# Moving a layer's modulation products from TensorE to VectorE, into three feed-forward stages

## What is computed

```
mod_lat = silu(c) @ w_mod + b_mod          # c: (1, 1024), w_mod: (1024, 6144)
mod_ctx = silu(c_ctx) @ w_mod + b_mod
sh1, sc1, g1, sh2, sc2, g2 = split(mod_lat, 6)
csh1, csc1, cg1, csh2, csc2, cg2 = split(mod_ctx, 6)
hx = modulate(rms_norm(x), sh1, sc1)
hc = modulate(rms_norm(ctx), csh1, csc1)   # with one layer nothing else of mod_ctx is used
```

## Time and profile before

| what | value |
|---|---|
| time, median of 3 runs | 2467.96 us (2465.76 to 2468.3) |
| span of the profiled execution, first to last instruction | 2465.7 us |
| mean granted clock of TensorE | 0.959 |
| PE busy | 2246.6 us, 91% |
| PEld busy | 2014.1 us, 82% |
| DVE busy | 979.8 us, 40% |
| ACT busy | 1157.1 us, 47% |
| POOL busy | 1191.6 us, 48% |

### The profile page before, as it was taken

One profiled execution on the slowest core, in us unless ns is written; L12 is line 12 of the kernel. 1 busy time (PEld: TensorE's weight loads), 2 busy tenths in 40 slices (PEclk: granted clock), 3 DMA queues, 4 the chain that ended last, 5 costly groups with the idle time before them and its releaser, 6 DMA issues. The chain is left out here.

```text
span 2465.7 us, 41821 instructions
## 1 busy us (share of the span) xinstructions
PE 2246.6 (91%) x17916; PEld 2014.1 (82%) x17916; DVE 979.8 (40%) x1980; ACT 1157.1 (47%) x1651; POOL 1191.6 (48%) x304
## 2 busy tenths in 40 slices
PE   8998989899998999888989999897987777998998
PEld 7998865488998999785568999775866777998997
DVE  2321644324211220356242321256665777333540
ACT  5433632465433442543255543455883555553342
POOL 6774610074875877440053887332310000675784
PEclk9999999899999999999989999898998888999999
DMA  7554522253654555432333554331204111653552
GB/s 251 171 175 130 155 83 86 69 173 101 201 170 143 189 183 162 139 111 86 120 103 103 171 188 154 118 104 52 69 21 135 35 36 24 209 165 126 180 180 95
DMA packets 303958, 318.49 MB, mean 129 GB/s; under 512 B 7881, under 2 KB 295101, under 8 KB 303261
## 3 DMA queue, kind: packets, MB, share of 16 engines
q1 hardware_dynamic: 303773, 315.81, 39.8%
HBM read 312.58 MB, written 3.21 MB: 128 GB/s over the span
## 5 line engine op out<-in xcount | busy, mean ns | idle before, releaser
L370 POOL TENSOR_TENSOR slab_lo<-ring,slab_hi 128x2048 fp32r<-128x2048 f32 (+1 forms) x238 | 1073.5, 4527 | 762.7 <-ACT slab_hi L359 727.0
L359 ACT CAST slab_hi<-ring 128x2048 fp32r<-128x2048 f32 (+1 forms) x238 | 443.8, 1869 | 550.8 <-PE bank L440 278.8
L435 PE MATMUL bank<-ffn_h_hi,slab_hi 128*128 128x256 f32 x1344 | 331.2, 284 | 0.0
L436 PE MATMUL bank<-ffn_h_lo,slab_hi 128*128 128x256 f32 x1344 | 329.7, 283 | 0.0
L435 PEld LDWEIGHTS bank<-ffn_h_hi,slab_hi 128*128 128x128 f32 x1344 | 257.9, 192 | 0.5 <-issue 0.3
L436 PEld LDWEIGHTS bank<-ffn_h_lo,slab_hi 128*128 128x128 f32 x1344 | 258.0, 192 | 0.1
L402 PE MATMUL bank<-ffn_hidden_hi,slab_hi 128*128 128x256 f32 x704 | 199.3, 283 | 0.0
L403 PE MATMUL bank<-ffn_hidden_lo,slab_hi 128*128 128x256 f32 x704 | 199.2, 283 | 0.0
L404 PE MATMUL bank<-ffn_hidden_hi,slab_lo 128*128 128x256 f32 x704 | 199.2, 283 | 0.0
L440 PE MATMUL bank<-ffn_h_hi,slab_lo 128*128 128x256 f32 x1344 | 189.1, 283 | 4.4 <-POOL slab_lo L370 4.4
L440 PEld LDWEIGHTS bank<-ffn_h_hi,slab_lo 128*128 128x128 f32 x1344 | 173.3, 192 | 5.2 <-POOL slab_lo L370 5.2
(11 more groups left out here) (655 smaller groups left out, 5369.0 us busy)
## 6 DMA issues: line engine op xcount, KB each, us to landing
ring<-in_ffn_w_in SPq DMA_DIRECT2D x88, 1024.0 KB, 5.1
ring<-in_ffn_w_out SPq DMA_DIRECT2D x32, 1024.0 KB, 5.2
ring<-in_w_in SPq DMA_DIRECT2D x27, 1024.0 KB, 5.3
ring<-in_mix_w_in SPq DMA_DIRECT2D x24, 1024.0 KB, 5.4
ring<-in_w_mod SPq DMA_DIRECT2D x24, 1024.0 KB, 5.2
ring<-in_w_up SPq DMA_DIRECT2D x22, 1024.0 KB, 5.1
ring<-in_ffn_w_out SPq DMA_DIRECT2D x16, 768.0 KB, 4.4
ring<-in_mix_w_out SPq DMA_DIRECT2D x8, 1024.0 KB, 5.2
```

Of the source, the lines that this page charges most:

```text
L359: act.copy(self.hi[i % self.PLACES][:, 0:w], K.ring[n % RING][:, 0:w]).then_inc(self.hi_ready, 1)
L370: pool.tensor_tensor(self.lo[i % self.PLACES][:, 0:w], place[:, 0:w], self.hi[i % self.PLACES][:, 0:w].bitcast(F32), ALU.subtract).then_in ...
L435: pe.matmul(out, w[0][:, k, col], act[0][:, k, :], start=(k == 0), stop=False)
L436: pe.matmul(out, w[0][:, k, col], act[1][:, k, :], start=False, stop=False)
```

## The change

The modulation slabs leave the layers' plan, and the attention and inverse stages lose all instructions of the old class. A new class reads w_mod in 16 pieces of 512 KB for each of three parts, during the second feed-forward stage of layer 0 (part 0), the first of layer 1 (part 1) and the second of layer 1 (part 2). DVE multiplies each group of a piece with one conditioning column as a scalar for each partition and adds it up in PSUM bank 7. Part 0 computes the first 2048 columns for both conditioning vectors, in pieces of four groups of 256 columns; parts 1 and 2 compute 2048 columns each for one vector, in pieces of two groups of 512. When all groups of some columns are added, DVE copies the bank to SBUF. At the stage's end PE sums these over the partitions by products with one column of ones, and DVE copies the result into `K.mod`. The issues are on SP's queue, between the slab loads, and each piece after the second waits until DVE has eaten the piece two before.

```
 class Modulations:
+    PIECES, PLACES = 16, 2
+    BANK = 7
+        self.both = part == 0
+        self.cols, self.groups = (HALF, 4) if self.both else (2 * HALF, 2)
+        self.a_group = KD // self.groups
+        self.count = self.PIECES // self.a_group
...
+    def sync(self, sync, p):
+        g, h = divmod(p, self.a_group)
+        if p >= self.PLACES:
+            sync.wait_ge(self.steps, self.eaten(p - self.PLACES))
+        src = groups_of(K.a["w_mod_2"], h * self.groups, self.groups, self.first * P + g * self.cols, self.cols)
+        sync.dma_start(self.place[p % self.PLACES][:, :, :], src).then_inc(self.landed[p % self.PLACES], 16)
...
+    def dve(self, dve, p):
+        dve.wait_ge(self.landed[p % self.PLACES], 16 * (self.landings + p // self.PLACES + 1))
+        for q in range(self.groups):
+            k, w = h * self.groups + q, self.place[p % self.PLACES][:, q, :]
+            for v in range(1 + self.both):
+                out = bank[:, v * self.cols:(v + 1) * self.cols]
+                if k == 0:
+                    last = dve.tensor_scalar(out, w, K.cs[:, k, v:v + 1], None, ALU.mult)
+                else:
+                    last = dve.scalar_tensor_tensor(out, w, K.cs[:, k, v:v + 1], out, ALU.mult, ALU.add)
+            if q < self.groups - 1:
+                own.after(dve, last)
+        last.then_inc(self.steps, 1)
+        dve.wait_ge(self.steps, self.eaten(p))
+        if h == self.a_group - 1:
+            dve.tensor_copy(self.sums[:, g, :], bank[:, :]).then_inc(self.steps, 1)
+            dve.wait_ge(self.steps, self.kept(g))
...
+    def pe(self, pe):
+        pe.wait_ge(self.steps, self.kept(self.count - 1))
+        for t in range(4 * self.count):
+            g, j = divmod(t, 4)
+            last = pe.matmul(bank[:, t:t + 1], self.sums[:, g, j * P:(j + 1) * P], K.c("ones", n=1), start=True, stop=True)
...
 def ffn_stage:
+                if mod is not None:
+                    for p in range(mod.PIECES):
+                        K.load_slabs(sync, n0 + 2 * p + RING + 1)
+                        mod.sync(sync, p)
                 K.load_slabs(sync, n0 + FK + 12 + RING)
...
                 ffn_out_pe(K, pe, split, hidden, x_updated, lambda: pe.wait_ge(product_ready, N))
+                if mod is not None:
+                    mod.pe(pe)
...
                             opening.dve(dve, i)
+                        if mod is not None:
+                            mod.dve(dve, i)
                 for jj in range(4):
+                    if mod is not None and jj < 3:
+                        for p in range(N + 2 * jj, min(N + 2 * jj + 2, mod.PIECES)):
+                            mod.dve(dve, p)
...
+                if mod is not None:
+                    mod.dve_end(dve)
 def layer_slabs:
-    slabs += [whole(K.a["w_mod_2"], l * (MOD_SLABS * HALF) + i * HALF) for i in range(MOD_SLABS)]
 rwkv_stage and attention_stage:
-                    mod.pe_first(pe)
-                    inv.act(act, between=lambda i: mod.act_first(act) if i == 1 else None)
+                    inv.act(act)
-                for _ in range(mod.AHEAD):
-                    mod.some(pe)
-                att.pe(pe, between=lambda: mod.some(pe), mid_step=lambda i: scan.pe(pe, i + EARLY))
-                mod.pe_end(pe)
+                att.pe(pe, mid_step=lambda i: scan.pe(pe, i + EARLY))
-                att.act(act, at_step=lambda i: (mod.act(act, i, att.CALLS), scan.act(act, i + EARLY - 1)))
-                mod.act(act, KD * MOD_SLABS, 1)
+                att.act(act, at_step=lambda i: scan.act(act, i + EARLY - 1))
-                mod.dve(dve)
```

More of the change, by code:

```diff
@@ L34 @@
 NEG = -1.0e30
-MOD_SLABS = 12
 LEVELS = (4, 5)
@@ L634, in all_tokens, with __init__, eaten, kept @@
         return self.rstd[:, :].unsqueeze(1).to_broadcast([P, n, T])
-def ffn_stage(K, tag, gain, opening=None):
+class Modulations:
+    PIECES, PLACES = 16, 2
+    BANK = 7
+    def __init__(self, K, ctx, part):
+        self.K, self.part = K, part
+        self.both = part == 0
+        self.cols, self.groups = (HALF, 4) if self.both else (2 * HALF, 2)
+        self.a_group = KD // self.groups
+        self.count = self.PIECES // self.a_group
+        self.first = 0 if self.both else 2 * KD * part
+        self.place = [K.sb(f"mod_piece{i}", [P, self.groups, self.cols], ctx=ctx) for i in range(self.PLACES)]
+        self.sums = K.sb("mod_sums", [P, self.count, 2 * HALF], ctx=ctx)
+        self.landed = [K.sem(f"mod_landed{i}") for i in range(self.PLACES)]
+        self.steps = K.sem("mod_eaten_kept_turned")
+        again = part == 2
+        self.landings = again * self.PIECES // self.PLACES
+        self.base = again * (self.PIECES + self.count + 1)
+    def eaten(self, p):
+        return self.base + p + 1 + p // self.a_group
+    def kept(self, g):
+        return self.base + (g + 1) * (self.a_group + 1)
+    def sync(self, sync, p):
+        K = self.K
+        g, h = divmod(p, self.a_group)
[4 more added lines that the diff above has]
+    def dve(self, dve, p):
+        K, own, bank = self.K, self.K.dve_own, self.K.bank[self.BANK]
+        g, h = divmod(p, self.a_group)
+        dve.wait_ge(self.landed[p % self.PLACES], 16 * (self.landings + p // self.PLACES + 1))
[15 more added lines that the diff above has]
+    def pe(self, pe):
+        K, bank = self.K, self.K.bank[self.BANK]
+        pe.wait_ge(self.steps, self.kept(self.count - 1))
+        for t in range(4 * self.count):
+            g, j = divmod(t, 4)
+            last = pe.matmul(bank[:, t:t + 1], self.sums[:, g, j * P:(j + 1) * P], K.c("ones", n=1), start=True, stop=True)
+        last.then_inc(self.steps, 1)
+    def dve_end(self, dve):
+        K, n = self.K, 4 * self.count
+        dve.wait_ge(self.steps, self.kept(self.count - 1) + 1)
+        if self.both:
+            dve.tensor_copy(K.mod[:, 0:n // 2, :].rearrange("p (g j) v -> p g j v", j=2),
+                            K.bank[self.BANK][:, 0:n].rearrange("p (g v j) -> p g j v", v=2, j=2))
+        else:
+            dve.tensor_copy(K.mod[:, self.first:self.first + n, 0], K.bank[self.BANK][:, 0:n])
@@ L639, in ffn_stage @@
+def ffn_stage(K, tag, gain, opening=None, mod_part=None):
     nc = K.nc
@@ L648, in ffn_stage @@
         split = Split(K, ctx, tag, n0, FK + 12)
+        mod = None if mod_part is None else Modulations(K, ctx, mod_part)
         gate_ready, silu_ready = K.sem(tag + "_gate_ready"), K.sem(tag + "_silu_ready")
@@ L1719, in rwkv_stage @@
         intra_ready, intra_read = K.sem("intra_ready"), K.sem("intra_read")
-        mod = Modulations(K, ctx)
         with ExitStack() as ictx:
@@ L1726, in _ @@
                 def _(sync):
-                    K.load_slabs(sync, mod.n0 + mod.FIRST + RING)
+                    K.load_slabs(sync, K.eaten + RING)
                 @block.tensor
@@ L1764, in _ @@
                     inv.pool(pool)
-        attention_stage(K, lt, xt, unit, mod)
+        attention_stage(K, lt, xt, unit)
 class RwkvScan:
@@ L1939, in act_root @@
         act.activation(flat(self.sq), flat(self.sq), ACT.Exp, scale=-0.5).then_inc(self.rstd_ready, 1)
[L1944 to L2020, removed]
@@ L2158, in softplus_small, with attention_stage @@
     return dve.tensor_scalar(out, q, 2.0, None, ALU.mult)
-def attention_stage(K, lt, xt, unit, mod):
+def attention_stage(K, lt, xt, unit):
     nc, s = K.nc, K.mx
@@ L2194, in attention_stage @@
         with nc.Block(no_gpsimd_drain=True) as block:
-            @block.sync
-            def _(sync):
-                K.load_slabs(sync, mod.n0 + MOD_SLABS + RING)
             @block.tensor
@@ L4126, in build @@
                 layer_start(K, l)
-                ffn_stage(K, "ffn1", K.col("ffn1_norm", KD))
+                ffn_stage(K, "ffn1", K.col("ffn1_norm", KD), mod_part=1)
             mixer(K, l)
             mix_xattn_stage(K, l)
-            ffn_stage(K, "ffn2", K.col("ffn2_norm", KD))
+            ffn_stage(K, "ffn2", K.col("ffn2_norm", KD), mod_part=2 * l)
             K.restart()
```

## The result

The change made the kernel slower: 2504.09 us, median of four runs, beside 2468.13 of the kernel before in the same comparison; ratio 1.0126, 95% interval 1.0098 to 1.0153. The forecast was 2433. The profiled execution took 2507.35 us, its span 2505.6, 39.9 more than before.

What follows compares the result with a forecast made beforehand. PE was taken to set the pace in attention steps and feed-forward stages. Layer 0 -26.7, layer 1 -22.5 and feed-forward ends +14.0 make -35.2 us, from 2467.96 to 2433 us; range for 8 in 10: 2418 to 2455.

Steps and rivals of the forecast that it cites:

- The clock: Attention steps without modulation products: mostly high clock, about 7 us low, costing 3.4 us a layer (bounds 0 and 26.5).
- The first rival: Clock stays at 1.2 GHz through all attention steps of both layers: +50 us on the sum, 2483 us, slower; 6%.
- Removed in the steps: Attention steps: 28 calls (56 modulation products) leave, 26.7 us; 35.3 us of other PE work remain, without waits.
- The head and the end: Before the steps, low clock from the rotation: +2.6 and +3.4 us; behind them, turns and copy removed: -2.6 a layer.
- Feed-forward loops and SP's queue: DVE's new products and 16 piece loads a stage fit beside PE and slabs, 3.0 us to spare: cost nothing.
- Stage ends: One-column products ending three feed-forward stages, 0.118 us a record: +7.2, +3.4, +3.4, together +14.0 us; 5.2 by the low bound.

Runs made afterwards that it cites:

- filled head: Changed kernel plus seven f32 products with unread results, before the wait for the normed q and k; 2490.39 us, 1.0061 to the kernel before.
- early form: Mixture of both kernels: eight modulation slabs per attention layer, two products at each call, so all in the first four steps; 2463.88 us, 0.9959.
- emptied head: Kernel before with AHEAD = 0: the sixteen modulation products between inverse and steps come later, in and behind the steps; 2506.29 us, 1.0127.
- ten fillers: Changed kernel with the filled head and one unread f32 product of 512 columns in each of the first ten steps; median 2492.66 us, 1.0036.
- spread form: Mixture of both kernels: eight modulation slabs per attention layer, one product at each call, spread over eight steps, rest on DVE; 2463.66 us, 0.9961.

## Why the prediction was wrong

**The clock.** This is the step that failed. Of bounds of 0 and 26.5 us a layer I took 3.4, "nearer to the rows of layer 1"; it was 28.2 (63.54 - 35.3), above even the bound, because the steps' work took 1.80 times as long at the low level and not 1.75. The rows chosen for it were the wrong ones: layer 1 kept the high level before with the modulation products in it, so that its rows said nothing of steps without them, and the run behind 457.8 was only a few microseconds, with the scan norm's products of 512 columns among them. Of the row counted against the change, 0.52 from 396 to 400, half was modulation products, at the end of a low stretch. The row that bore on it lies just ahead, in the trace of the kernel before. From 382 to 394 PE runs no modulation product there, and in layer 0 the level falls at 389.5, after 2.3 us without a wait (in layer 1 the same products kept it, so this row shows that it can fall and not that it must):

```profile
387.20:389.50 2.30, 2.30 (x19) 1.58 (x20) 2.12 (x4) 0.00 (x0) 0.00 (x0) 1.00 0.00 0
389.60:394.10 4.50, 4.50 (x20) 3.70 (x18) 2.43 (x4) 0.00 (x0) 0.00 (x0) 0.50 0.01 2
```

The runs put in its place: without the modulation products the steps don't hold the high level (63.54 us at 0.50; falls at 426.5 with the filled head and behind the products of the early form); with them the level comes back and stays (71.6 and 71.7 us with the emptied head), and long products whose result nobody reads do the same if there are enough of them. The first rival, given 6%, had the outcome and nearly the size of the steps (61.8 us a layer, 63.54 measured; 2483 forecast by it, 2504 measured).
The Trainium skill (TensorE: Matmul & The Clock Gate, "What's actually happening") has the clock set by how busy PE has been recently, and the default throttled. The low level behind the 7.49 us gap agrees; but here PE shows as busy in all of 63.54 us at 0.50, and the measurement decides: a busy PE in the profile is no sign of the high level.

**Removed in the steps.** Right: no L1988, no wait in PE's place, 35.3 us of other work. With ten fillers at the high level the steps took 45.7 us, which is 35.3 and ten times 1.04.

**The head and the end.** The low level at the rotation came as forecast, but the head lost 6.6 and 7.4 us instead of 2.6 and 3.4, since the level did not come back before the first scores and the inverse began late and low too (3.68 us for its first 64 records). Behind the steps the 2.6 us of turns were saved and more than lost: the mean product took 3.78 us instead of 1.98, and the row sums behind it ran low for most of their time.

**Feed-forward loops and SP's queue.** Right: +1.5 us in three stages, though two figures were off. A piece lands in 6.1 us and not in 2.6. Its size alone is not the reason, since two slabs of 512 KB landed in 3.7; in the loop SP issues each piece 0.4 us behind a slab of 1024 KB:

```profile
641.70 0.37 SPq L268 DMA_DIRECT2D ring<-in_ffn_w_in  x1
642.11 0.58 SPq L675 DMA_DIRECT2D mod_piece<-in_w_mod  x1
mod_piece<-in_w_mod SPq DMA_DIRECT2D x48, 512.0 KB, 6.1
ring<-in_mix_w_in SPq DMA_DIRECT2D x2, 512.0 KB, 3.7
```

And the gate waited for a product of DVE four times, 3.5 us, and DVE waited 20.1 us for pieces between 600 and 783. Neither reached PE.

**Stage ends.** Right in mechanism, and the price of a record was nearly right at the high level; it was again the clock that was missed. In the spread form 32 of these records ran at 1.00 from end to end, 0.11 us each, below the 0.118 taken (the records, then stretches with PEclk third from the end):

```profile
1537.06 3.63 PE L703 MATMUL bank<-const,mod_sums 128*128 128x1 f32 x32
1537.06:1540.70 3.64, 3.63 (x34) 3.55 (x32) 0.76 (x2) 0.00 (x0) 0.00 (x0) 1.00 0.00 0
789.79:798.95 9.16, 9.16 (x66) 9.07 (x64) 0.76 (x2) 0.00 (x0) 0.00 (x0) 0.77 0.01 2
```

In the changed kernel (last row) the level falls during them, behind loops that had run at 1.00, and the 64 records take 0.143 us each: 15.9 us for the three ends and not 14.0. The norm behind them ends late by another 1.5 and 1.3 us at two of the three. Some 3.5 us between the places are not traced further. Two small sums of the prediction are off without consequence: 3.4 less 0.9 is 2.5 and not 2.6, and by the 0.057 us of the turns the three ends are 6.2 us and not 5.2.

## What to carry to other kernels

Work taken from TensorE has two prices: its own time, and what it does for the clock of the products around it. Before such work leaves a stretch, look for rows of what remains, alone, with PE busy: if any of them is low, cost the whole rest at the low level and make that the forecast. If the high level needs something among short products, let it be work that the program owes anyway, spread over the whole stretch: here 24 modulation products over eight steps, with two fillers ahead of them, took 49.3 us where 56 products had taken 62 to 65.4 and none 63.5. And one profiled execution is one sample: with ten fillers the runs of a single kernel lay 68 us apart.

## What was not expected of the hardware

The granted clock fell from 1.00 to 0.50 in the middle of a stretch in which PE had no idle time at all (at 426.5 with the head filled, near 428 and 1196 with the products early). The same program's two layers ran the same steps once at 0.52 and once at 1.00, 79.9 and 45.7 us. And a DMA of 512 KB, issued 0.4 us behind one of 1024 KB, landed in 6.1 us, where slabs of 512 KB elsewhere in the same execution landed in 3.7 and 3.9 and those of 1024 KB in 5.0 to 5.4.
